# Gates and branch projections with tokens on partitions in a hybrid RWKV/attention/pooling block: 512 moving columns per matmul

## What is computed

```
h = rms_norm(x, norm1_g)
proj = h @ w_in                       # 1024 x 6912: RWKV (1792), attention (1536), pool (512), gates (3072)
y_rwkv = rwkv7_time_mix(p_rwkv, ...)  # 8 heads x 64, chunked here: triangular inverse in levels
y_attn = moba_attention(rms_norm(q), rms_norm(k), v)   # 8 heads x 64, one block: causal, ALiBi
y_pool = pool_mix(p_pool, pool_w, pool_scale)
branch = einsum('btnc,ncd->btnd', [y_rwkv, y_attn, y_pool], w_branch)
gates = sigmoid(p_gate)               # 3 x 1024
x = x + sum_n(gates * branch) @ w_out
h2 = rms_norm(x, norm2_g)
x = x + square(relu(h2 @ w_ff1)) @ w_ff2
```

## Time and profile before

| | |
|---|---|
| median of 3 runs | 497.81 us (497.4 to 497.96) |
| the profiled execution, its own time | 499.51 us |
| its span in the profile | 497.7 us |
| PE busy, matmuls | 482.8 us (97%), 3936 |
| DVE busy | 307.3 us (62%) |
| ACT busy | 239.3 us (48%) |
| GpSimd busy | 45.5 us (9%) |
| weight splits on DVE, L1052 | 138 x 1.252 us |
| weight splits on ACT, L831 | 138 x 1.048 us |
| one core's DMA, mean | 154 GB/s |

### The profile page before, as it was taken

How to read it: one execution, slowest core, us unless ns; L and a number is a source line. 1 busy time by engine, 2 the same in 40 slices (tenths; PEclk the granted TensorE clock), 3 DMA queues, 4 the chain that set the end, 5 groups by cost and what they waited for, 6 DMA issues and landing times.

```text
span 497.7 us, 9337 instructions
## 1 busy us (share of the span) xinstructions
PE 482.8 (97%) x3936; PEld 436.9 (88%) x3936; DVE 307.3 (62%) x447; ACT 239.3 (48%) x357; POOL 45.5 (9%) x48
## 2 busy tenths in 40 slices
PE   3999999999999999999999999999999999999997
PEld 3989986677999889999999988899999999999995
DVE  3656898944573778565338996766565555555542
ACT  6577542455652536456333254654454445444440
POOL 1001002320670011100001500000000000000000
PEclk9999999999999999999999999999999999999999
DMA  8985553354422342643324648377666566656612
GB/s 246 267 233 155 155 144 110 96 160 128 129 87 85 87 129 85 189 128 120 99 80 128 206 136 237 106 242 205 184 186 194 170 182 203 197 183 190 190 41 84
DMA packets 95515, 76.85 MB, mean 154 GB/s; under 512 B 2545, under 2 KB 85105, under 8 KB 95474
## 3 DMA queue, kind: packets, MB, share of 16 engines
q1 hardware_dynamic: 95474, 76.26, 51.7%
HBM read 75.20 MB, written 1.05 MB: 153 GB/s over the span
## 4 chain that ended last, share of the span: by engine, by line
PE 86%; DVE 6%; DMA 3%; issue 2%; ACT 2%; POOL 1%; SPq 0%; ACTq 0%; DVEq 0%
PE bank L473 24%; PE bank L474 23%; PE bank L475 23%; DVE w_lo L1052 2%; DMA stage<-in_w_ff 2%; PE bank L565 2%; POOL small L1373 1%; DMA stage<-in_w_in 1%; ACT w_hi L831 1%; PE bank L691 1%; PE bank L707 1%; PE bank L669 1%; PE bank L742 1%; PE bank L731 1%; PE bank L741 1%
## 5 line engine op out<-in xcount | busy, mean ns | idle before, releaser
L1052 DVE TENSOR_TENSOR w_lo<-stage,w_hi 128x1024 fp32r<-128x1024 f32 x138 | 172.2, 1252 | 123.8 <-ACT w_hi L831 123.6
L831 ACT CAST w_hi<-stage 128x1024 fp32r<-128x1024 f32 x138 | 143.9, 1048 | 120.1 <-PE bank L475 87.5
L473 PE MATMUL bank<-h_hi,w_hi 128*128 128x256 f32 x592 | 173.0, 292 | 1.6 <-DVE h_lo L1076 1.4
L474 PE MATMUL bank<-h_lo,w_hi 128*128 128x256 f32 x592 | 168.5, 285 | 0.0
L475 PE MATMUL bank<-h_hi,w_lo 128*128 128x256 f32 x592 | 168.3, 284 | 0.0
L473 PEld LDWEIGHTS bank<-h_hi,w_hi 128*128 128x128 f32 x592 | 114.3, 193 | 5.7 <-issue 3.3
L474 PEld LDWEIGHTS bank<-h_lo,w_hi 128*128 128x128 f32 x592 | 114.4, 193 | 0.7
L475 PEld LDWEIGHTS bank<-h_hi,w_lo 128*128 128x128 f32 x592 | 114.3, 193 | 0.0
L473 PE MATMUL bank<-w_hi,r_hi 128*128 128x512 f32 x128 | 50.0, 391 | 0.0
L474 PE MATMUL bank<-w_lo,r_hi 128*128 128x512 f32 x128 | 50.0, 391 | 0.0
L475 PE MATMUL bank<-w_hi,r_lo 128*128 128x512 f32 x128 | 49.8, 389 | 0.0
(11 more groups left out here) (207 smaller groups left out, 623.9 us busy)
## 6 DMA issues: line engine op xcount, KB each, us to landing
stage<-in_w_ff SPq DMA_DIRECT2D x64, 512.0 KB, 4.2
stage<-in_w_in SPq DMA_DIRECT2D x54, 512.0 KB, 3.9
stage<-in_w_branch SPq DMA_DIRECT2D x12, 512.0 KB, 3.6
stage<-in_w_out SPq DMA_DIRECT2D x8, 512.0 KB, 4.7
xs<-in_x SPq DMA_DIRECT2D x2, 512.0 KB, 3.9
out<-xs SPq DMA_DIRECT2D x4, 256.0 KB, 2.1
cst<-in_consts SPq DMA_DIRECT2D x1, 897.0 KB, 8.0
lora<-in_g_up SPq DMA_DIRECT2D x1, 256.0 KB
```

Source lines behind the costliest of these rows:

```text
L473: pe.matmul(o, lh, rh, start=first, stop=False)
L474: pe.matmul(o, lh, rl, start=False, stop=False)
L831: nc.scalar.copy(w_hi[:, v % RING], stage[:, v % STAGES]).then_inc(hi_done, 1)
L1052: dve.tensor_tensor(w_lo[:, v % RING], stage[:, v % STAGES], w_hi[:, v % RING].bitcast(F32), ALU.subtract)\
```

## The change

Gate units become tok units: 128 tokens stationary, 512 gate columns moving, two units (the two halves of the contraction) for each pair of results. Branch units keep their number, and now have the tokens of a branch result stationary and 512 weight columns moving; their weight pieces become 256 rows x 512 columns where they were 512 x 256. Gates, branch results and their sum thus have tokens on partitions, so that the sum has to be transposed before the output projection. This is `turned_place`: four groups of four transposes on PE (L829 of the changed kernel), behind quarters 1 and 2 of unit 32 and 1 and 3 of unit 33, from which ACT and DVE take the high and low parts directly out of the bank. The turning of q and k moves from quarter 1 to quarter 2 of units 10 and 12. The gates' results go round banks 0 to 2; from unit 13 to unit 26 attention, pool and the rest share one ring of five banks (3 to 7). Branch units and the output units swap their pairs of banks. The second weight split of unit 32 comes behind its `finish`.

```diff
-UNITS += [("feat", N_RWKV + N_ATTN + N_POOL + 256 * q) for q in range(12)]
+GATES_AT = N_RWKV + N_ATTN + N_POOL
+UNITS += [("tok", GATES_AT + 512 * g, kh) for g in range(6) for kh in range(2)]
...
-    turn, count, signalled, ring = {}, [0] * 8, [0] * 8, [0]
+    turn, count, signalled, ring = {}, [0] * 8, [0] * 8, [4, 5, 6, 7]
...
+        if t == S_HEAD:
+            ring.insert(0, 3)
+        if t == S_BR:
+            ring.remove(3)
...
+                elif u[0] == "tok" and u[2] == 0 and u[1] >= GATES_AT:
+                    g = (u[1] - GATES_AT) // 512
+                    for tt in range(TT):
+                        use(("tok", u[1], tt), (2 * g + tt) % 3, dense=tt == 1)
...
-                    b = 2 * ((t - S_BR + 1) % 2)
-                    use(("unit", t, 0), b, dense=True)
+                    b = 2 * ((t - S_BR) % 2)
+                    use(("unit", t, 0), b)
...
-                        use(("out", u[2], tt), 2 * (1 - u[2]) + tt, dense=tt == 1)
+                        use(("out", u[2], tt), 2 * u[2] + tt, dense=tt == 1)
...
+def turned_place(t, p):
+    return {(S_OUT - 1, 1): (0, 0), (S_OUT - 1, 2): (0, 1), (S_OUT, 1): (1, 0), (S_OUT, 3): (1, 1)}.get((t, p))
...
-    if t in S_TURN and p == 1:
+    if t in S_TURN and p == 2:
...
-            out += [(("pt", g, e), 2 + e) for e in range(2)]
+            out += [(("pt", g, e),) for e in range(2)]
...
-            out += [(("score", g, e), 2 + e) for e in range(2)]
+            out += [(("score", g, e),) for e in range(2)]
... (PE, branch unit)
-                    for k in range(W // P):
-                        ins = mm3(o[:, T * i:T * i + T], wh[:, k, P * i:P * i + P], wl[:, k, P * i:P * i + P],
-                                  rh[:, k0 + k], rl[:, k0 + k], k == 0, k == W // P - 1)
+                    name = ("unit", t, i)
+                    o = room(pe, name) if p < 2 else ps(name)
+                    for kk in range(2):
+                        k = 2 * (p // 2) + kk
+                        ins = mm3(o[:], lh[:, k0 + k, P * i:P * i + P], ll[:, k0 + k, P * i:P * i + P],
+                                  wh[:, kk], wl[:, kk], k == 0, k == 3)
... (PE, output unit)
-                        if i == 0:
-                            pe.wait_ge(m_ready, 2 * u[1] + p // 2 + 1)
+                        if p < 2:
+                            copied(pe, ("mt", u[1], i))
... (PE, extra)
+                if turned_place(t, p):
+                    ch, tt = turned_place(t, p)
+                    pe.wait_ge(m_pre, 2 * ch + tt + 1)
+                    o = room(pe, ("mt", ch, tt))
+                    for k in range(4):
+                        ins = pe.transpose(o[:, P * k:P * k + P], gates[ch][:, tt, P * k:P * k + P], ident)
... (ACT and DVE, extra)
+                    nc.scalar.mul(y_hi[:, 4 * ch:4 * ch + 4, P * tt:P * tt + P], o[:].rearrange("p (k t) -> p k t", k=4), 0.5)\
+                    dve.scalar_tensor_tensor(out=y_lo[:, 4 * ch:4 * ch + 4, P * tt:P * tt + P], in1=part, scalar=0.5,
+                                             in0=o[:].rearrange("p (k t) -> p k t", k=4), op0=ALU.mult, op1=ALU.subtract)\
... (ACT and DVE, the list of unit t)
-                late = t == S_FF - 1
+                late = t in (S_OUT - 1, S_FF - 1)
```

More of the change, by code:

```diff
@@ L228, in dense_ends @@
         for tt in range(TT):
-            if u[0] == "branch":
-                ends[("unit", t, tt)] = 2 * t + 1 + tt
+            if u[0] == "branch" and tt == 1:
+                ends[("unit", t, 1)] = 2 * t + 2
         if u[0] == "tok" and u[2] == 1:
@@ L990, in finish @@
                         nc.scalar.activation(sq_att[tt], o[:], ACT.Square).then_inc(qk_sq, 1)
+                elif S_GATE <= t < S_BR:
+                    if u[2] == 1:
+                        for tt in range(TT):
+                            name = ("tok", u[1], tt)
+                            o = take(act, name)
+                            nc.scalar.activation(gates[(t - S_GATE) // 2][:, tt], o[:], ACT.Tanh, scale=0.5)\
+                              .then_inc(drained_of(name), 1)
                 elif t == S_VA + 1:
@@ L995, in finish @@
                         nc.scalar.copy(vatt[:, tt], o[:]).then_inc(drained_of(name), 1)
-                elif S_GATE <= t < S_BR:
-                    o = take(act, ("unit", t))
-                    nc.scalar.activation(gates[(t - S_GATE) // 2][:, t % 2 ^ S_GATE % 2], o[:], ACT.Tanh, scale=0.5)\
-                      .then_inc(drained_of(("unit", t)), 1)
-                elif u[0] == "branch" and u[1] == 0:
-                    for i in range(2):
-                        m = 2 * u[2] + i
-                        act.wait_ge(m_pre, m + 1)
-                        nc.scalar.mul(y_hi[:, 2 * m:2 * m + 2], gates[u[2]][:, i].rearrange("p (k t) -> p k t", k=2), 0.5)\
-                          .then_inc(m_hi, 1)
                 elif t in (S_POOL, S_POOL + 1):
```

65 lines of the change are left out of this document (35 added, 30 removed).

## The result

The changed kernel takes 499.77 us, median of 20 runs (498.62 to 502.17). The kernel before, run beside it, takes 498.92 us (20 runs, 497.40 to 501.04), 1.1 us more than its first three runs had shown. The ratio is 1.0019, 95% interval 1.0010 to 1.0028: slower by 0.95 us, within the 0.2% that count as no change. The forecast was 497.0 us, 0.85 us faster than before, with a range up to 499.2.

A forecast was written before the change was run, and what follows sets the result against it. PE bounds the kernel: number of matmuls times their spacing, plus a few stands. Terms -3.2 + 0.35 - 1.3 - 0.15 + 0.6 + 1.9 + 0.95 = -0.85 gave a median of 497.0 us, range 494.2 to 499.2.

The forecast's parts named there:

- from the gates to the output projection: First branch matmul to output projection: PE stands 3.1 us in unit 32 for DVE's add; +1.9 us.
- From there the path is fixed: Behind unit 32's stand: transposes and quarters of 0.41, 1.44, 0.5 and 1.45 us, output projection starting at 291.5.
- a rival with 14%: Unit 32: PE's clock falls to half pace in the stand, costing +2.1 us, so 499.1; 14%.
- Gates: Units 15 to 26: wide matmuls replace pairs of narrow ones at a quicker pace; -3.2 us.
- Where DVE leads: Inside the gates, units 19 to 21: nine quarters of PE lie in DVE's chain and gain nothing; +0.6 us.
- The Trainium skill's rule that I weighed: Gates: gap of N / 2.4 + 2.5 ns gives some 0.7 us, not 3.2, ending near 499.5; given no chance.
- unit 15's bank: Start of unit 15, the first gate unit: PE waits for ACT's copy of unit 14 from bank 0; +0.35 us.
- unit 12: Turning q and k one quarter later: PE no longer stands before the second four transposes; -1.3 us.
- unit 10: Turning q and k one quarter later: the stall only moves, as small matmuls need DVE's L1190 pair; -0.15 us.
- the output projection's transposes: Output projection: two more groups of four transposes beside wide matmuls, 0.47 us each; +0.95 us.
- PE not held: Unit 32: DVE led by PE or loads, so the wait shrinks; 3.0 us less, 494.0; 14%.
- New bank waits: Five shared banks, DVE behind PE in units 17 and 18: one or two waits cost 1 to 2 us, 498.5; 12%.

The follow-up runs named there:

- e1_fill: Changed kernel with twelve unneeded 512-column matmuls put in front of PE's wait at unit 32; 0.9993 of the kernel before.
- e6_bank: Changed kernel with unit 14 in bank 2 instead of bank 0; 1.0007 of the kernel before.
- e7_halves: Changed kernel with each wide matmul of the gates, but the one that begins a bank, issued as two of 256 columns; 1.0061 of the kernel before.
- e5_turn: Changed kernel with the turns in units 10 and 12 put back behind quarter 1; 1.0026 of the kernel before.
- e8_warm_before: Kernel before the change with eleven matmuls on ones ahead of PE's first wait; 1.0009 of the kernel before.
- e9_warm_after: Changed kernel with eleven matmuls on ones ahead of PE's first wait; 1.0012 of the kernel before.
- e2_order: Changed kernel with DVE's splits of pieces 67 to 70 moved behind unit 31's multiplies and adds; 1.0053 of the kernel before.
- e3_order_sum: As e2_order, but GpSimd's second sum also waits until DVE's adds of unit 31 are done; 1.0037 of the kernel before.
- e15_start: Changed kernel with sums on DVE, unit 14 in bank 2, splits of pieces 67 to 70 reordered, and PE's starting waits filled with matmuls; 0.9952 of the kernel before.

## Why the prediction was wrong

**The term "from the gates to the output projection"** carries the error. Up to PE's restart it was right: the stand is 3.00 us (3.1), caused by the chain of DVE and GpSimd that I had read from the earlier trace rows, put down to DVE's add, in front of the transposes of unit 32. The sentence that failed is "From there the path is fixed: four transposes 0.41, a quarter 1.44, four transposes 0.5, a quarter 1.45". PE took 5.3 us for it (283.08 to 288.38) instead of 3.8, since the clock fell. I had this as a rival with 14%, priced at +2.1; e1_fill prices it at 1.59 in the profile and 1.3 in the runs. What the fall does was rightly described and its chance much too small. Its condition was not right: I had let it decide "as soon as the stand is long enough", and the same stand of 3.00 us had the fall in after and not in e6_bank. I had argued that no gap of this length stood in the trace to say where it decides. That was a reason for even odds, not for one in seven, and the one sentence of the Trainium skill that I cited for it (an idle gap between bursts brings the lower clock back) was the better guide here: it came behind four of the five stands of 3.0 us at this place that the profiles show.

**Gates.** -3.2 was -2.5 (twelve times 0.21), as the pace between small matmuls is nearer the slow rows; "Where DVE leads", +0.6, was +0.4. Together -2.08 for -2.6, and e7_halves shows that it is all pace. The Trainium skill's rule that I weighed (0.7 us for the gates by its back-to-back issue gap) is not borne out: 2.0. The same section gives that formula for a matmul by itself and says that in a stream the weight loads count too; this kernel is such a stream, and I had left that out.

**The small terms** held: unit 15's bank +0.43 for +0.35 (e6_bank takes it away), unit 12 -1.1 for -1.3 and unit 10 nothing for -0.15 (e5_turn), the output projection's transposes +0.55 for +0.95. Of that, pieces 66 and 67, where the transposes stand, have +0.74, and piece 72 -0.25; piece 72 takes 3.76 us in before and 4.21 in e8_warm_before without an edit there, so its part can't be put down to the change.

**The sum.** Of the 2.1 us between forecast and profile, 1.6 are the clock, 0.5 the gates, and the rest (unit 12, against the transposes) cancels. Put together with a fall in four executions out of five, the profile's stretches give 1.25 - 0.2 x 1.59 = +0.93, and the runs gave +0.95. The agreement is closer than it can mean: the share of four in five comes from five profiles, one of each of five kernels, and the runs' interval is 0.45 us either way. The absolute number was off by another 1.1 us, because before's first three runs lay at the low end of its range of 3.6 us.

**Rivals.** PE not held: refuted, DVE's multiply of unit 31 came 32.19 us after the first branch matmul (249.37 to 281.56), 32.18 in before. New bank waits: none above 0.2 us.

## What to carry over

Where an edit makes the leading engine quicker into a wait that it doesn't move, look at how long it will then stand, and price what follows on that engine, not only the stand. A split or load that is held back in one engine's list to let urgent work by also holds back its buffer, and the wait comes back some pieces later in front of other work: move the one that has an idle stretch to go to, and trace its buffer to the next user. An operation given to a helper engine is only free if it doesn't slow the engine that it relieves; here the busy engine did the sum itself in less time than it lost beside the helper.

## What the runs showed of the hardware

Unexpected was how unsteady the clock's fall is. In the profiles of kernels with PE standing 3.0 to 3.5 us late in the program, the granted clock went to 0.50 at five of seven stands: after, e5_turn, e7_halves and e9_warm_after at unit 32, e2_order at piece 70 (3.45 us); not in e6_bank (3.00) nor in e3_order_sum (3.16). It never did at unit 32 in the ten profiles where the wait at unit 32 was at most 1.55 us or filled. The slow rows don't always begin at the same place: in after the transposes of 283.08 still took 0.41 us and the rows behind them were slow; in e5_turn and e7_halves the transposes themselves took 0.77 us from start to start. A window behind e6_bank's stand, for comparison with after's 0.52:

```profile
286.00:288.00 2.00, 2.00 (x12) 1.66 (x11) 2.00 (x3) 0.78 (x2) 0.00 (x0) 1.00 0.29 113
```

At the start the half pace appears with a granted clock of 1.00 in before and of 0.50 in others (e6_bank, 14 to 16 us), so a reading of 1.00 is no proof of full pace there. In e15_start the clock fell at 45 us with no stand ahead of it: the longest wait in the 30 us before was 0.34 us.
